# Queueing exponentials and their products only when their inputs are nearly due, and the linear attention's preparations in stages

## What is computed

```python
def hybrid_layer(x, mem, ...):
    h = rms_norm(x, g_mix)
    (q, k_c, v_c, k_s, v_s, k_w, v_w, g_logit,
     q_l, k_l, v_l, a_l, r_l) = jnp.split(h @ w_in, split_points(), axis=-1)
    o_nsa = nsa_mixer(...)            # compressed, selected and windowed attention, 8 heads
    log_a = jax.nn.log_sigmoid(a_l @ w_gk2 + b_gk) / GLA_GATE_NORM
    o_gla = gla_mixer(q_l * GLA_DK ** -0.5, k_l, v_l, log_a)      # 4 heads
    o_gla = rms_norm(o_gla, g_gla_out) * jax.nn.silu(r_l)
    x = x + jnp.concatenate([o_nsa, o_gla], axis=-1) @ w_out
    ...                               # cross attention to mem, then a gated feed-forward
def gla_mixer(q, k, v, log_a):        # per chunk of 64 tokens
    b = jnp.cumsum(ac, axis=2)
    decay = jnp.exp(jnp.where(causal, b[:, :, :, None, :] - b[:, :, None, :, :], -jnp.inf))
    attn = jnp.einsum('bhid,bhjd,bhijd->bhij', qc, kc, decay)
    ...
```

## Time and profile before

| | |
|---|---|
| three runs | 2476.28, 2476.84, 2477.47 us (median 2476.84) |
| the profiled execution's own time | 2474.57 us |
| its span, first to last instruction | 2473.2 us |
| TensorE's mean granted clock | 0.990 of full speed |
| read from HBM | 448.99 MB, 182 GB/s over the span |
| busy: PE, DVE, ACT | 97%, 61%, 45% of the span |

### The profile page before, as it was taken

How to read it: one execution, slowest core, us unless ns; L and a number is a source line. 1 busy time by engine, 2 the same in 40 slices (tenths; PEclk the granted TensorE clock), 3 DMA queues, 4 the chain that set the end, 5 groups by cost and what they waited for, 6 DMA issues and landing times.

```text
span 2473.2 us, 28654 instructions
## 1 busy us (share of the span) xinstructions
PE 2411.4 (97%) x11302; PEld 1992.0 (81%) x11302; DVE 1500.7 (61%) x2117; ACT 1109.0 (45%) x1388; POOL 0.2 (0%) x4
## 2 busy tenths in 40 slices
PE   8999999999999999999999997898999999999999
PEld 7888888888888888888788776687888888888887
DVE  4565999865544555577567576476655555554443
ACT  4444444544444444454446454344544444443333
POOL 0000000000000000000000000000000000000000
PEclk9999999999999999999999998899999999999999
DMA  7645666656665776575545443253566666666664
GB/s 266 193 156 168 194 189 194 213 179 213 195 195 155 255 228 192 181 229 182 166 152 175 161 144 131 88 169 117 187 188 189 187 191 191 187 191 192 201 201 143
DMA packets 124227, 452.99 MB, mean 183 GB/s; under 512 B 13691, under 2 KB 15916, under 8 KB 123068
## 3 DMA queue, kind: packets, MB, share of 16 engines
q1 hardware_dynamic: 124092, 451.17, 58.3%
HBM read 448.99 MB, written 2.12 MB: 182 GB/s over the span
## 4 chain that ended last, share of the span: by engine, by line
PE 95%; DVE 3%; ACT 1%; DMA 1%; issue 0%; SPq 0%; ACTq 0%; DVEq 0%
PE ps L453 88%; PE ps L325 1%; DVE t_wlo L394 1%; PE ps L585 1%; PE ps L535 1%; ACT t_whi L393 1%; PE ps L1399 1%; PE ps L568 1%; PE ps L499 0%; PE ps L975 0%; PE ps L1521 0%; DMA t_raw<-w_out 0%; PE ps L434 0%; DVE t_st L472 0%; DMA t_raw<-w_kv 0%
## 5 line engine op out<-in xcount | busy, mean ns | idle before, releaser
L453 PE MATMUL ps<-t_whi,t_A 128*128 128x512 f32 (+1 forms) x4992 | 1554.0, 393 | 27.0 <-DVE t_wlo L394 12.9
L394 DVE TENSOR_TENSOR t_wlo<-t_raw,t_whi 128x1024 fp32r<-128x1024 f32 x805 | 980.6, 1224 | 873.7 <-ACT t_whi L393 868.0
L393 ACT ACTIVATE t_whi<-t_raw 128x1024 fp32r<-128x1024 f32 x805 | 849.0, 1058 | 1120.6 <-PE ps L453 1107.8
L453 PEld LDWEIGHTS ps<-t_whi,t_A 128*128 128x128 f32 x4992 | 929.5, 189 | 219.1 <-DVE t_wlo L394 14.3
L453 PE MATMUL ps<-t_wlo,t_A 128*128 128x512 f32 (+1 forms) x2496 | 973.6, 390 | 0.0
L453 PEld LDWEIGHTS ps<-t_wlo,t_A 128*128 128x128 f32 x2496 | 471.2, 189 | 98.7
L453 PE MATMUL ps<-t_whi,t_Y0a 128*128 128x512 f32 x1152 | 356.0, 390 | 0.0
L453 PEld LDWEIGHTS ps<-t_whi,t_Y0a 128*128 128x128 f32 x1152 | 215.2, 188 | 44.3 <-DVE t_wlo L394 0.3
L453 PE MATMUL ps<-t_wlo,t_Y0a 128*128 128x512 f32 x576 | 224.3, 389 | 0.0
L453 PEld LDWEIGHTS ps<-t_wlo,t_Y0a 128*128 128x128 f32 x576 | 108.1, 188 | 22.6
L869 DVE SCALAR_TENSOR_TENSOR t_Y1a<-t_H,t_pp,t_Y1a 128x255 f32<-128x255 f32 (+29 forms) x240 | 96.2, 463 | 0.0
(11 more groups left out here) (291 smaller groups left out, 1101.0 us busy)
## 6 DMA issues: line engine op xcount, KB each, us to landing
t_raw<-w_in SPq DMA_DIRECT2D x376, 512.0 KB, 4.1
t_raw<-w_gu SPq DMA_DIRECT2D x176, 512.0 KB, 3.6
t_raw<-w_down SPq DMA_DIRECT2D x88, 512.0 KB, 4.2
t_raw<-w_branch SPq DMA_DIRECT2D x64, 512.0 KB, 4.2
t_raw<-w_out SPq DMA_DIRECT2D x64, 512.0 KB, 3.7
t_raw<-w_ck SPq DMA_DIRECT2D x16, 512.0 KB, 3.6
t_raw<-w_cv SPq DMA_DIRECT2D x16, 512.0 KB, 4.4
t_raw<-w_cq SPq DMA_DIRECT2D x8, 512.0 KB, 3.6
```

What stands on the lines that cost most here:

```text
L393: a = S.do(lambda e: e.activation(whi[:, s, 0:n], raw[:, d % NR, 0:n], ACT.Copy), tok, free)
L394: b = V.do(lambda e: e.tensor_tensor(wlo[:, s, 0:n], raw[:, d % NR, 0:n], whi[:, s, 0:n].bitcast(F32), ALU.subtract), a, free)
L453: fn = lambda e, x=x, w=w, kt=kt, k=k, t=t, j=j, bk=bk: e.matmul(bk[:, 0:n], x[:, u["k0"] + kt, t * P:(t + 1) * P], w[:, k, :], start=(kt ...
```

## The change

A second rule, `near`, lets a thread go on when what it reads is due in at most 0.5 us. `attend` asks it before it queues its exponentials. `prelude` and `weigh` become generators with a `yield` between differences, exponentials and products; `some()` looks at the first three entries of `ahead`, takes the first whose token is nearly due, queues one stage of it and returns. No instruction is added or removed on any engine; only the order changes.

```diff
+NEAR = 0.5
+    def near(*toks):
+
+        while max([due(x) for x in toks]) > T.now + NEAR:
+            yield
...
             c.v(lambda e: e.tensor_scalar(nm, mx, -1.0, None, ALU.mult), n=8)
+        yield from near(c.tok)
         fns = [lambda e, h=h: e.activation(L3[:, h, :], src[:, h, :], ACT.Exp, bias=nm[:, h:h + 1],
...
             c.tok = behind
-            c.s(*exps)
+            e1 = c.s(*exps)
             c.tok = behind
             c.v(*fns)
-            c.s(lambda e: e.activation(kpr[:, 384:768], kpr[:, 384:768], ACT.Exp),
-                lambda e: e.activation(q12[:], q12[:], ACT.Exp))
+            yield c.tok
+            e2 = c.s(lambda e: e.activation(kpr[:, 384:768], kpr[:, 384:768], ACT.Exp),
+                     lambda e: e.activation(q12[:], q12[:], ACT.Exp))
+            yield [e1, e2]
...
+            yield c.tok
             c.s(lambda e: e.activation(all_, all_, ACT.Exp), n=o)
+            yield c.tok
             c.v(*[lambda e, i=i, w=w: e.tensor_tensor(w, w, q3[:, :, i:16], ALU.mult) for i, w in w3.items()],
...
         def some():
 
-            if ahead:
-                kept = c.tok
-                ahead.pop(0)()
-                c.tok = kept
+            for job in ahead[:3]:
+                if due(job[1]) <= T.now + NEAR:
+                    kept = c.tok
+                    c.tok = job[1]
+                    job[1] = next(job[0], None)
+                    if job[1] is None:
+                        ahead.remove(job)
+                    c.tok = kept
+                    return
 
         def plan(h, behind):
-            ahead.append(lambda: prelude(h, behind))
+            ahead.append([prelude(h, behind), T.last()])
             for j in range(len(COLS)):
-                ahead.append(lambda j=j: weigh(h, j))
+                ahead.append([weigh(h, j), T.last()])
```

## The result

| | before | changed |
|---|---|---|
| runs, median (us) | 2476.61 (2476.28 to 2477.47) | 2498.14 (2497.82 to 2502.06) |
| ratio to before | | 1.0091, 95% interval 1.0079 to 1.0103 |
| the profiled execution, its span | 2474.57, 2473.2 | 2497.82, 2496.5 |
| TensorE's mean granted clock | 0.990 | 0.983 |

The change makes the kernel 0.9% slower; a second measurement gave 1.0099 (1.0086 to 1.0113). The forecast was 2496, inside 2476 to 2514.

A forecast was written before the change was run, and what follows sets the result against it. TensorE was taken as the bound, busy for 2411.4 of 2473.2 us. New costs A to E of 70 us less 51 gained gave +19, so 2496 us, range 2476 to 2514.

The forecast's parts named there:

- The long stretch: Sign: about 75 us with no L458 ahead of `w_out2`'s first product, VectorE busy for two thirds of it.
- the wait at `ck1`: Sign: first column sum (L1414) waits about 8 us on products (L1346) that stand behind a split.
- the 3.9 us behind L1402: Sign: a wait of 4 us behind L1402, the copy of head 2.
- B: At `ck1`, head 1's late preparations make TensorE wait: 10.6 us, bounds 6 and 14.
- D: Between `cv1` and `w_out2`, all of head 3 without weight products: 75 us long, excess 48, bounds 24 and 53.
- E: TensorE restarts at the lower clock after B, C and D: three at 2.3 us, 7 us.
- What before paid: From `ck1` to `w_out2`'s first product, idle time 32 us and low clock 19 us go: 51 us gained.
- A: Head 0's copy stands one copy and one split later in ScalarE's list: 0.6 us.
- C: Head 2's copy stands behind table loads, exponentials and a copy, 7.2 us, partly covered by TensorE: 4.1 us.
- Rival 1: Faster: hand-offs hide in the stretch behind `cv1`, its excess 22 us; -7, so 2470 us; chance 0.08.
- Rival 2: No change: one long pause costs what eight short ones did; 2477 us; chance 0.11.
- Rival 3: Worse: all TensorE's pieces in B to D run at 1.2 GHz; +32, so 2509 us; chance 0.21.

The follow-up runs named there:

- head 1 alone: Changed kernel with all due stages taken at a call, except head 1's, taken one a call; 2485.0 us, 1.0036 of the kernel before.
- more calls: Changed kernel with `some()` called at every step of the linear attention: 2473.6 us with one stage a call, 2467.5 with all due stages.

## Why the prediction was right, and where its terms were off

*The mechanism was right.* The time was 2498.1 for 2496, a change of +21.5 for +19. The long stretch, the wait at `ck1`, the 3.9 us behind L1402, the disappearance of the L311 and L1135 waits: each is in rows above or below. The experiments with head 1 alone and with more calls show the cause that the forecast named, that a stage is taken only at a call of `some()`. What it did not see is how much the question whether a stage is due adds to this, and that the loss would be half as large without the attention's wait. That the sum came so close is partly luck: B and D were too large and E too small by amounts that nearly cancel.

*What before paid, 51 us:* from its three windows, idle time 14.3 + 7.5 + 11.2 and low clock 0.06 x 139.9 + 0.24 x 13.95 + 0.09 x 76.76 = 18.7, less the 0.8 that both have: 50.9. Right, though shares of whole windows also count the low clock where TensorE was idle, some 2 us here.

*A:* L1402 at head 0 waits 2.10 us for 1.58: +0.5, forecast 0.6. A wait of 1.15 us behind a split some 37 us later was not foreseen.

*B, forecast 10.6:* 2.21 + 5.28 = 7.5 in the trace; the 0.6 for the copy did not show. The order was as described, and here is the timeline of it:

```profile
1405.09 0.32 PE L1379 MATMUL ps<-t_Y0b 128*128 128x384 bf16 x1 [2.21 <-DVE t_Y0b L1322]
...
1407.93 4.50 PE L416 MATMUL ps<-t_raw,t_Y0b 128*32 128x256 f32 x40
...
1409.07 12.34 SPq L146 DMA_DIRECT2D t_raw<-w_in  x9
...
1412.73 1.06 ACT L398 ACTIVATE t_whi<-t_raw 128x1024 fp32r<-128x1024 f32 x1 [1.91 <-DMA t_raw<-w_in]
...
1413.81 1.23 DVE L399 TENSOR_TENSOR t_wlo<-t_raw,t_whi 128x1024 fp32r<-128x1024 f32 x1 [6.18 <-ACT t_whi L398]
...
1414.96 1.33 DVE L1344 TENSOR_TENSOR t_Y1b<-t_Y1b,t_H 128x256 f32<-128x256 f32 x4
1416.32 1.33 DVE L1346 TENSOR_TENSOR t_Y1b<-t_Y1b,t_H 128x256 f32<-128x256 f32 x4
...
1417.70 3.46 PE L1414 MATMUL ps<-t_Y1b,t_cc 128*128 128x256 f32 x8 [5.28 <-DVE t_Y1b L1346]
```

From the transfer's issue to the copy 3.66 us passed, where I took the 5.0 of the earlier trace rows, and of TensorE's 4.5 us of narrow products 3.4 lay behind the issue, not 2.2.

*C, forecast 4.1:* 3.87. *D, forecast 75 us:* 73.4, of which VectorE works 47.2 (51) and waits 26.2 (24); the excess over 27 us of warm products is 46.4 (48). The 27 is the forecast's estimate; the trace's 43.6 us at a clock of 0.64 would be 28 at full speed. My 51 us of VectorE's work were 4 too many and its waiting 2 too few.

*E, forecast 7, is the term that was mis-sized.* Behind D it is 0.05 x 46.68 = 2.3 us, a restart at the price I took. But from 1397 to 1526 the clock is 0.92 over 128.9 us, 10.3 us, where two restarts at 2.3 were counted. Windows of the changed kernel show where it was low, with 1.00 between these pieces:

```profile
1406.10:1412.93 6.83, 6.33 (x69) 2.95 (x68) 1.20 (x4) 3.16 (x5) 0.00 (x0) 0.50 0.67 226
...
1416.34:1423.17 6.83, 5.47 (x14) 4.60 (x15) 6.83 (x13) 2.33 (x3) 0.00 (x0) 0.50 0.82 287
...
1457.30:1460.71 3.41, 3.41 (x10) 2.64 (x9) 0.07 (x1) 1.14 (x2) 0.00 (x0) 0.50 0.02 8
...
1494.85:1498.26 3.41, 3.12 (x12) 2.83 (x13) 2.87 (x9) 0.24 (x1) 0.00 (x0) 0.50 0.22 85
```

B is two waits (2.21 and 5.28 us), and the clock is low behind each of them, where I counted one restart. By half of TensorE's busy time these two pieces cost 3.2 and 2.7 us, and the one behind C 1.6. The piece at 1457 costs 1.7 and follows no wait: ahead of it TensorE was busy throughout, at the last with short products (L1414, L1536, L504). What lowered the clock there was not tried by itself. So E is 9.2 + 2.3 = 11.5 us over busy time, and 12.6 over whole windows, which is how the 50.9 were taken. With 12.6 the account is 0.5 + 1.15 + 7.5 + 3.9 + 46.4 + 12.6 and one more wait of 1.1 us, 73.2; less 50.9 that is +22.3 of the measured 23.3. One us is not accounted for.

*The range.* The forecast's own 2487 to 2507 doesn't follow from the bounds named with it: D at 40 and B at 6 together give 2483. The measured time lies inside either.

*The rivals.* Rival 1 (the hand-offs hide) needed a stretch under 56 us. Rival 2 (nothing moves) needed B near 6.6, which came close, and 13 us of waiting in D, where 26 stood. Rival 3 (TensorE at 1.2 GHz throughout) had something in it: the clock of 0.64 in the stretch is mostly the lower level, but raising it from 0.60 to 0.81 by the fillers shortened the stretch by 3.7 us only. What full speed would give was not reached.

## What to carry to other kernels

Cutting background work into stages that are queued only when due takes waiting instructions out of the way of what stands behind them, but each stage then needs a call of its own, at a time when it is due: where the calls are as few as before, the work ends later, and what is left when the stream runs out of products is paid in full. Count the chances to queue against the stages, and let a chance take all that is due; here the same two edits with a `while` in the place of an `if` and no `return` turned 0.9% slower into 0.4% faster. Test such parts together: the attention's wait was worth nothing on the kernel before, cost 11 us with one stage a call, and gained 12 us with all.

## What the hardware showed that was not expected

Filling the waits of the stretch with products of zeros raised its granted clock from 0.60 to 0.81, with 57.0 instead of 45.2 us busy in it, and not to full speed; the kernel's own products then took some 13 us less, and the stretch was 3.7 us shorter. In the changed kernel the clock also fell to 0.50 at 1457, ahead of which TensorE had no wait. Six L458 at the head of the next unit took 2.93 us at a restart in the changed kernel, as after the short pauses of before, though a stretch of 73 us at a clock of 0.64 lay ahead of them.

```profile
1599.44 2.93 PE ps L458 x6
...
1603.23 1.85 PE ps L458 x6
```
